# A decoder trunk on one core: the six matmuls of a dense chunk, ordered by column half in place of halves in turn

## Chip, cores and metric

The kernel runs on one NeuronCore of one Trainium2 chip. The metric is the device time of one execution in microseconds (us), smaller is better. The time before is the median of three runs, 2590.06 us (2585.79 to 2590.27).

## What is computed

One inference step of a two-layer trunk, on 512 prompt tokens and 8 x 4 new tokens of running sequences, width 1024, all in float32. Cut to what matters:

```python
for l in range(DEPTH):                                # 2 layers
    x = x + 0.5 * swiglu(rmsnorm(x), ffn1)            # 1024 -> 2816 -> 1024
    z = rmsnorm(x) @ w_in[l]                          # 1024 -> 3144
    # three head groups read z: short convolution, causal pooling,
    # and sparse attention with a top-k indexer (paged cache for the new tokens)
    x = x + concat(y_conv, y_pool, y_attn) @ w_o[l]   # 1024 -> 1024
    x = x + 0.5 * swiglu(rmsnorm(x), ffn2)
y = rmsnorm(x)
```

The dense products are the feed-forward networks (two per layer, each with gate, up and down), `w_in` and `w_o`.

## The kernel before, in words

All tokens, 512 + 32 = 544 of them, are the columns of every dense product (`TOK = 544`, `HT = 272`). Activations lie transposed, one chunk of 128 channels on the 128 partitions, so one output tile of 128 channels is the sum over 8 chunks (2 in the down projection) of a 128 x 128 weight block times a 128 x 544 chunk of activations. 544 columns do not fit one PSUM bank of 512 floats, so a tile is a pair of banks, the left half (columns 0 to 271) in one and the right half (272 to 543) in the next. `pair(p)` is that view; there are four pairs, p = 0 to 3.

Precision: weights and activations are split into a high and a low part of the reduced type fp32r (`w_hi`, `w_lo`, `h_hi`, `h_lo`, `act_hi`, `act_lo`). ScalarE makes the high part of a weight unit (L576), GpSimd the low part (L832), VectorE the low part of the activations (L1010, L1029). A chunk is then three products that are added up in PSUM: high weights by high activations, high weights by low activations, low weights by high activations.

The function `product` (L1273 to L1279) issues them: three products, each on two halves, six matmuls per chunk. In the code before, the outer loop runs over the products and the inner one over the halves (`hf`). Every dense product of the kernel goes through it:

- `unit_tile` (L1285): 8 chunks of one tile, for most gate and up tiles and for `w_in`.
- `gate_up` (L1318) with `again` false: the first tiles of a network, two tiles side by side, chunk by chunk as the normalised activations arrive (`h_chunk`, L1281, waits ahead of a chunk).
- `down` (L1338): 2 chunks per tile, 8 tiles per block of 256 hidden channels.
- the first tiles of `w_in`, and `out_part` for `w_o`.

A network has 11 blocks of 256 hidden channels; each block is 4 gate and up tiles of 8 chunks and 8 down tiles of 2 chunks. So one network calls `product` 11 x (32 + 16) = 528 times, `w_in` 26 x 8 = 208 times, `w_o` 8 x 8 = 64 times. Over two layers that is 2 x (2 x 528 + 208 + 64) = 2656 calls.

The order of work is written out by hand, engine by engine. Waits stand ahead of `product`, never inside it. Only the last of the six matmuls can carry an increment, of the semaphore `tiles`, and it does where the chunk is the last of its tile. The readers of a tile (L617 and L1024, L1036, L670, L1256) wait for that increment and read both halves of the pair in one instruction.

Line 1277 is the matmul in `product`, so all dense matmuls stand under that line in the profile. For each, the hardware has a weight load of its own (engine PEld) and the matmul (engine PE).

Of the kernel before, what the change touches and what calls it, by code (L numbers as in the profile page):

```python
# [175 lines left out]
def trunk(nc, a):  # L176

    ctx = ExitStack()
    with ctx:
# [1085 lines left out]
        def _(pe):  # L1265
# [6 lines left out]

            def product(out, w0, w1, xh, xl, first, last):  # L1273

                for w, x in ((w0, xh), (w0, xl), (w1, xh)):
                    for hf in range(2):
                        ins = pe.matmul(out[:, hf, :], w, x[:, HT * hf:HT * (hf + 1)],  # L1277
                                        start=first and w is w0 and x is xh, stop=last and w is w1)
                return ins  # L1279
# [5 lines left out]
            def unit_tile(c, p, ks, wait_h=None, first=True, last=True):  # L1285

                wh, wl = (w[:, c % 6, 0:P * len(ks)].rearrange("p (k n) -> p k n", k=len(ks)) for w in (w_hi, w_lo))
                for n, k in enumerate(ks):
                    if wait_h is not None:
                        h_chunk(wait_h, k)  # L1290
                    ins = product(pair(p), wh[:, n, :], wl[:, n, :], h_hi[:, k, :], h_lo[:, k, :],
                                  first and n == 0, last and n == len(ks) - 1)
                return ins
# [18 lines left out]
            def ffn(l, f):  # L1312
# [5 lines left out]
                def gate_up(i, j, c0, again):  # L1318

                    if not again:  # L1320

                        split_ready(l, ph, j, 1)
                        for k in range(KC):
                            h_chunk(nh, k)
                            for p in range(2):
                                wh, wl = (w[:, p, P * k:P * (k + 1)] for w in (w_hi, w_lo))
                                ins = product(pair(p), wh, wl, h_hi[:, k, :], h_lo[:, k, :], k == 0, k == KC - 1)
                                if k == KC - 1:
                                    ins.then_inc(tiles, 1)
                    for p in range(0 if again else 2, 4):  # L1330
                        split_ready(l, ph, j, c0 + p)
                        if again:

                            pe.wait_ge(silu_done if p < 2 else gu_done, s0 + 2 * i + p % 2 - 1)
                            pe.wait_ge(x_updates, xb + 8 * i - 11 + p)
                        unit_tile(c0 + p, p, range(KC)).then_inc(tiles, 1)

                def down(i, j, c0, final):  # L1338
                    split_ready(l, ph, j, c0 + 1)
                    pe.wait_ge(act_ready, s0 + 2 * i + 2)  # L1340
                    for c in range(KC):
                        p = c % 4
                        if c >= 4 or final:
                            pe.wait_ge(x_updates, xb + 8 * i + c - 3)
                        else:
                            pe.wait_ge(silu_done if p < 2 else gu_done, s0 + 2 * i + 3 + p % 2)
                        for m in range(2):
                            wh, wl = (w[:, (c0 + m) % 6, c * P:(c + 1) * P] for w in (w_hi, w_lo))
                            ins = product(pair(p), wh, wl, act_hi[:, m, :], act_lo[:, m, :], m == 0, m == 1)
                        ins.then_inc(tiles, 1)  # L1350
# [382 lines left out]
```

## Time and profile before

| | |
|---|---|
| median of three runs | 2590.06 us |
| the profiled execution, its own time | 2589.05 us |
| its span, first to last instruction | 2587.3 us |
| mean granted TensorE clock | 0.959 |
| PE busy, weight loads busy | 93%, 88% of the span |
| VectorE, ScalarE, GpSimd busy | 37%, 29%, 36% |
| share of L1277 in the chain that ended last | 78% |
| DMA | 264.64 MB, mean 102 GB/s |

Start from the shares of the engines, then ask the chain that ended last, which tells whose work sets the end. Busy times of matmuls overlap (each record lasts longer than the distance to the next), so the time per matmul is read from starts: a stretch of the chain and its count, or the distance between two rows of the timeline.

### The profile page before, as it was taken

What the parts mean: (1) busy time and instruction counts of PE and PEld (TensorE: products, weight loads), DVE (VectorE), ACT (ScalarE), POOL (GpSimd) and SP (SyncE); (2) the same over time, 40 slices, a digit from 0 to 9 for tenths busy, and PEclk for the clock granted to TensorE, in tenths of its full rate; (3) what the DMA queues carried; (4) which work ended last, traced back from release to release, by engine and by line L of the source; (5) the groups of instructions that cost most, each with busy time, mean ns of one, the idle gap of its engine ahead of it and who ended that gap; (6) DMA issues with size and microseconds to landing.
All of it is one profiled execution on the core that took longest, in us unless ns stands there. A gap on an engine that the chain in (4) does not pass through costs nothing.

```text
span 2587.3 us, 53036 instructions
## 1 busy us (share of the span) xinstructions
PE 2414.1 (93%) x19355; PEld 2270.0 (88%) x19355; DVE 956.6 (37%) x1714; ACT 757.7 (29%) x1140; POOL 925.2 (36%) x491
## 2 busy tenths in 40 slices
PE   4699999899988999999989999989998999999997
PEld 2699999859965899999989999987896668999996
DVE  2122222469746222222242222244984632222223
ACT  1322222342244232222242222234224433222223
POOL 0433443316600344333434433332562033444331
PEclk6899999899989999999989999989999988999998
DMA  4333332212379423222313323321236852233221
GB/s 89 95 96 96 105 95 73 61 41 80 98 230 288 128 82 89 73 89 89 98 53 106 96 83 94 90 69 50 58 97 203 268 181 64 84 97 97 73 87 45
DMA packets 340192, 264.64 MB, mean 102 GB/s; under 512 B 35086, under 2 KB 291560, under 8 KB 340040
## 3 DMA queue, kind: packets, MB, share of 16 engines
q1 hardware_dynamic: 338512, 260.14, 33.7%
q10 hardware_dynamic: 1032, 2.62, 0.9%
q8 instruction: 78, 1.28, 0.2%
q14 instruction: 58, 0.48, 0.1%
q0 software_dynamic: 512, 0.13, 0.0%
HBM read 253.12 MB, written 9.89 MB: 102 GB/s over the span
## 4 chain that ended last, share of the span: by engine, by line
PE 87%; SPq 4%; DMA 3%; DVE 2%; issue 2%; ACT 1%; DVEq 0%; ACTq 0%; POOLq 0%
PE ps L1277 78%; SPq L463 2%; DMA raw<-in_ffn_gate 2%; PE ps L1539 2%; PE ps L1459 1%; SPq L460 1%; PE ps L1638 1%; PE ps L1557 1%; PE ps L1627 1%; DVE work_p L1103 1%; DMA vp<-in_cache_v 1%; PE ps L1619 1%; PE ps L1381 1%; PE ps L1445 0%; PE ps L1596 0%
## 5 line engine op out<-in xcount | busy, mean ns | idle before, releaser
L832 POOL TENSOR_TENSOR w_lo<-raw,w_hi 128x1024 fp32r<-128x1024 f32 (+1 forms) x336 | 793.1, 2376 | 1512.3 <-ACT w_hi L576 1507.6
L1277 PE MATMUL ps<-h_hi,w_hi 128*128 128x272 f32 x3904 | 805.6, 291 | 59.8 <-DVE h_lo L1010 57.3
L1277 PE MATMUL ps<-h_lo,w_hi 128*128 128x272 f32 x3904 | 803.3, 290 | 0.8 <-DVE cat L1185 0.8
L1277 PE MATMUL ps<-h_hi,w_lo 128*128 128x272 f32 x3776 | 779.4, 288 | 0.0
L1277 PEld LDWEIGHTS ps<-h_hi,w_hi 128*128 128x128 f32 x3904 | 611.4, 190 | 62.6 <-DVE h_lo L1010 58.1
L1277 PEld LDWEIGHTS ps<-h_lo,w_hi 128*128 128x128 f32 x3904 | 616.6, 191 | 3.5 <-issue 3.5
L1277 PEld LDWEIGHTS ps<-h_hi,w_lo 128*128 128x128 f32 x3776 | 596.9, 190 | 0.0
L576 ACT ACTIVATE w_hi<-raw 128x1024 fp32r<-128x1024 f32 (+1 forms) x336 | 342.4, 1041 | 251.7 <-DMA raw<-in_ffn_gate 215.0
L1024 DVE TENSOR_TENSOR gated<-ps,silu 128x544 f32<-128x544 f32 x88 | 63.8, 724 | 917.9 <-PE ps L1277 917.9
L1036 DVE SCALAR_TENSOR_TENSOR xT<-ps,xT 128x544 f32<-128x544 f32 x352 | 255.0, 725 | 266.3 <-PE ps L1277 265.0
L1277 PE MATMUL ps<-act_hi,w_hi 128*128 128x272 f32 x1408 | 292.8, 289 | 9.5 <-DVE act_lo L1029 9.5
L1277 PE MATMUL ps<-act_lo,w_hi 128*128 128x272 f32 x1408 | 291.8, 288 | 0.0
L1277 PE MATMUL ps<-act_hi,w_lo 128*128 128x272 f32 x1408 | 289.2, 286 | 0.0
L623 ACT ACTIVATE act_hi<-gated 128x544 fp32r<-128x544 f32 x88 | 53.5, 651 | 628.5 <-PE ps L1277 593.0
L1277 PEld LDWEIGHTS ps<-act_hi,w_hi 128*128 128x128 f32 x1408 | 220.2, 189 | 10.4 <-issue 10.4
L1277 PEld LDWEIGHTS ps<-act_lo,w_hi 128*128 128x128 f32 x1408 | 222.1, 189 | 0.0
L1277 PEld LDWEIGHTS ps<-act_hi,w_lo 128*128 128x128 f32 x1408 | 221.6, 189 | 0.0
L617 ACT ACTIVATE silu<-ps 128x544 f32<-128x544 f32 x88 | 55.0, 625 | 343.2 <-PE ps L1277 343.2
L1539 PE MATMUL ps<-cst,kp 128*128 128x128 f32 x512 | 71.3, 294 | 19.1 <-DMA kp<-in_cache_k 19.1
L753 ACT ACTIVATE keysT<-ps 128x512 f32<-128x512 f32 x96 | 55.3, 597 | 102.5 <-PE ps L1539 102.5
L1539 PEld LDWEIGHTS ps<-cst,kp 128*128 128x128 f32 x512 | 60.6, 150 | 27.9 <-issue 24.4
L1126 DVE MAX8 top<-work_s 32x8 f32<-32x1032 f32 x64 | 78.4, 1224 | 10.1 <-DVE work_s L1122 1.1
(214 smaller groups left out, 1625.0 us busy)
## 6 DMA issues: line engine op xcount, KB each, us to landing
raw<-in_ffn_gate SPq DMA_DIRECT2D x88, 512.0 KB, 3.8
raw<-in_ffn_up SPq DMA_DIRECT2D x88, 512.0 KB, 4.0
raw<-in_ffn_down SPq DMA_DIRECT2D x88, 512.0 KB, 3.4
kp<-in_cache_k SPq DMA_DIRECT2D x128, 256.0 KB, 3.1
vp<-in_cache_v SPq DMA_DIRECT2D x128, 256.0 KB, 4.3
raw<-in_w_in SPq DMA_DIRECT2D x48, 512.0 KB, 3.8
raw<-in_w_o SPq DMA_DIRECT2D x16, 512.0 KB, 6.5
kipages<-in_cache_kidx SPq DMA_DIRECT2D x128, 32.0 KB, 1.8
```

The costliest lines, as they stand in the source:

```text
L460: page = sp.value_load(pt_sb[0:1, at_:at_ + 1], min_val=0, max_val=last_page)
L463: sp.dma_start(dst[:, q, :], src[l, page, :, :]).then_inc(s, 16)
L576: act.activation(w_hi[:, c % 6, 0:n], raw[:, c % 3, 0:n], ACT.Copy).then_inc(units_hi, 1)
L617: act.activation(halves(silu[:, m, :]), pair(m), ACT.Silu).then_inc(silu_done, 1)
L623: act.activation(act_hi[:, m, :], gated[:, m, :], ACT.Copy).then_inc(acthi_done, 1)
L753: act.activation(dst, ps[:, RING_BANKS[RING_NO[name] % NRB], 0:n], ACT.Copy).then_inc(ring_act, 1)
L832: pool.tensor_tensor(w_lo[:, c % 6, 0:n], raw[:, c % 3, 0:n], w_hi[:, c % 6, 0:n].bitcast(F32), ALU.subtract).then_inc(units_split, 1)
L1024: dve.tensor_tensor(halves(gated[:, m, :]), pair(2 + m), halves(silu[:, m, :]), ALU.mult).then_inc(gu_done, 1)
L1036: dve.scalar_tensor_tensor(halves(xT[:, c, :]), pair(c % 4), 0.5, halves(xT[:, c, :]), ALU.mult, ALU.add).then_inc(x_updates, 1)
L1126: dve.max(top8[0:32, 0, :], work_s[:, :]).then_inc(topk, 1)
L1277: ins = pe.matmul(out[:, hf, :], w, x[:, HT * hf:HT * (hf + 1)], start=first and w is w0 and x is xh, stop=last and w is w1)
L1539: ins = pe.transpose(ps[:, bank, P * c:P * (c + 1)], kp[slot][:, q, P * c:P * (c + 1)], ident)
```

## The change

The two loops of `product` change places. All three products of the left half are issued first, then all three of the right. The matmuls, their operands, their number, the start and stop flags of each, and the last matmul of the six are the same.

```diff
             def product(out, w0, w1, xh, xl, first, last):
 
-                for w, x in ((w0, xh), (w0, xl), (w1, xh)):
-                    for hf in range(2):
+                for hf in range(2):
+                    for w, x in ((w0, xh), (w0, xl), (w1, xh)):
                         ins = pe.matmul(out[:, hf, :], w, x[:, HT * hf:HT * (hf + 1)],
                                         start=first and w is w0 and x is xh, stop=last and w is w1)
                 return ins
```

On TensorE, the first tile of the down projection (`ps` is PSUM, `act_hi` and `act_lo` the parts of the gated activations) stood like this before, `x2` being the left and the right half:

```order
249 L1340 ISA [waits units_split]
250 L1346 REGISTER_ALU [waits act_ready]
251 L1277 MATMUL ps<-act_hi,w_hi 128x272 [waits silu_done]
252 L1277 MATMUL ps<-act_hi,w_hi 128x272
253 L1277 MATMUL ps<-act_lo,w_hi 128x272 x2
254 L1277 MATMUL ps<-act_hi,w_lo 128x272 x2
255 L1277 MATMUL ps<-act_hi,w_hi 128x272 x2
```

At the same place in the changed program:

```order
427 L1340 ISA [waits units_split]
428 L1346 REGISTER_ALU [waits act_ready]
429 L1277 MATMUL ps<-act_hi,w_hi 128x272 [waits silu_done]
430 L1277 MATMUL ps<-act_lo,w_hi 128x272
431 L1277 MATMUL ps<-act_hi,w_lo 128x272
432 L1277 MATMUL ps<-act_hi,w_hi 128x272
433 L1277 MATMUL ps<-act_lo,w_hi 128x272
434 L1277 MATMUL ps<-act_hi,w_lo 128x272
```

The waits stand where they stood. Rows 429 to 431 are the left half, rows 432 to 434 the right. The other four engines' programs are the same, row for row.

## Rows read from the trace of the kernel before

**Rows 1.** The page, busy time, share of the span and instructions of TensorE.

```profile
span 2587.3 us, 53036 instructions
...
PE 2414.1 (93%) x19355; PEld 2270.0 (88%) x19355; DVE 956.6 (37%) x1714; ACT 757.7 (29%) x1140; POOL 925.2 (36%) x491
```

**Rows 2.** The page, granted clock of TensorE in 40 slices, in tenths.

```profile
PEclk6899999899989999999989999989999988999998
```

**Rows 3.** The page, chain that ended last, by engine and by line.

```profile
PE 87%; SPq 4%; DMA 3%; DVE 2%; issue 2%; ACT 1%; DVEq 0%; ACTq 0%; POOLq 0%
PE ps L1277 78%; SPq L463 2%; DMA raw<-in_ffn_gate 2%; PE ps L1539 2%; PE ps L1459 1%; SPq L460 1%; PE ps L1638 1%; PE ps L1557 1%; PE ps L1627 1%; DVE work_p L1103 1%; DMA vp<-in_cache_v 1%; PE ps L1619 1%; PE ps L1381 1%; PE ps L1445 0%; PE ps L1596 0%
```

**Rows 4.** The chain in order of time: start us, us, what.

```profile
84.67 386.66 PE ps L1277 x3072
...
579.67 72.36 PE ps L1277 x576
```

**Rows 5.** L1277 by operands: count, duration ns min/median/max, first and last start us.

```profile
L1277 PE MATMUL ps<-h_hi,w_hi x3904: 283/288/596, 84.7 to 2533.3; 128*128 128x272 f32 x196
...
L1277 PE MATMUL ps<-h_lo,w_hi x3904: 282/288/595, 85.3 to 2533.5; 128*128 128x272 f32 x196
...
L1277 PE MATMUL ps<-h_hi,w_lo x3776: 282/286/432, 85.7 to 2533.8; 128*128 128x272 f32 x199
...
L1277 PE MATMUL ps<-act_hi,w_hi x1408: 286/288/428, 135.2 to 2559.9; 128*128 128x272 f32 x176
...
L1277 PE MATMUL ps<-act_lo,w_hi x1408: 283/288/428, 135.4 to 2560.2; 128*128 128x272 f32 x176
...
L1277 PE MATMUL ps<-act_hi,w_lo x1408: 282/286/428, 135.7 to 2560.4; 128*128 128x272 f32 x176
...
L1277 PE MATMUL ps<-h_lo,w_lo x128: 286/289/428, 852.7 to 2145.3; 128*128 128x272 f32 x128
```

**Rows 6.** Timeline of PE inside a down projection: start us, us, what.

```profile
1000.33 0.41 PE L1277 MATMUL ps<-act_lo,w_hi 128*128 128x272 f32 x2
1000.58 0.41 PE L1277 MATMUL ps<-act_hi,w_lo 128*128 128x272 f32 x2
1000.83 0.42 PE L1277 MATMUL ps<-act_hi,w_hi 128*128 128x272 f32 x2
1001.09 0.41 PE L1277 MATMUL ps<-act_lo,w_hi 128*128 128x272 f32 x2
1001.34 0.41 PE L1277 MATMUL ps<-act_hi,w_lo 128*128 128x272 f32 x2
```

**Rows 7.** One stretch: us, busy (count) of each engine, granted clock, DMA.

```profile
950.00:1250.00 300.00, 300.00 (x2402) 300.00 (x2402) 69.52 (x97) 70.81 (x85) 123.58 (x52) 1.00 0.30 91
```

**Rows 8.** Timeline of PE in the first chunks of `w_in`, granted clock 0.50.

```profile
498.69 0.66 PE L1277 MATMUL ps<-h_lo,w_hi 128*128 128x272 f32 x2
499.15 0.66 PE L1277 MATMUL ps<-h_hi,w_lo 128*128 128x272 f32 x2
499.60 0.66 PE L1277 MATMUL ps<-h_hi,w_hi 128*128 128x272 f32 x2
```

**Rows 9.** Timeline of PE in the index scores, 344 columns, then the line's durations.

```profile
576.33 3.05 PE L1464 MATMUL ps<-srelu,wsel 128*32 128x344 f32 x10
...
L1464 PE MATMUL ps<-srelu,wsel x24: 449/452/453, 576.0 to 1821.7; 128*32 128x344 f32 x24
```

**Rows 10.** Timeline of PE in the key transposes, 128 columns, then the line's durations.

```profile
766.15 1.04 PE L1539 MATMUL ps<-cst,kp 128*128 128x128 f32 x8
...
L1539 PE MATMUL ps<-cst,kp x512: 272/273/449, 708.7 to 2053.7; 128*128 128x128 f32 x171
```

**Rows 11.** What PE waited for: us in total, times, longest us.

```profile
PE ps L1277 <- DVE h_lo L1010: 57.3, 6, 44.7
...
PE ps L1277 <- DVE act_lo L1029: 9.5, 4, 2.4
```

## The prediction

> **What bounds the kernel now.** I read the shares of the engines first. TensorE is busy 93% of the span, and it has as many weight loads as matmuls, 19355 of each [rows 1]. A busy share alone can be an engine that waits in the right places, so the chain that ended last comes next: 87% of it is TensorE, and line 1277, the matmul of `product`, has 78% by itself [rows 3], some 2010 us. Whatever changes the time of one of these matmuls changes the time of the kernel, nearly one for one.
>
> How many are they? The seven groups by operands add up to 3 x 3904 - 128 + 3 x 1408 + 128 = 15936 [rows 5], which is 6 x 2656, the calls of `product` counted in the code.
>
> How long is one? Not the 288 ns of its record: records overlap. In the timeline of a down projection each pair of matmuls starts 0.25 or 0.26 us after the one ahead [rows 6], so 125 ns each. Over 300 us at full clock there are 2402 of them, 124.9 ns [rows 7]. The first 3072 of the chain take 386.66 us, 125.9 ns with the few waits among them, and the 576 of `w_in` take 125.6 ns [rows 4]. I call this distance from start to start the pitch. At half clock (1.2 GHz) pairs start 0.45 or 0.46 us apart [rows 8], 227 ns each, which is 272 columns at one per cycle, 226.7 ns, and nothing on top. At full clock (2.4 GHz) 272 columns would be 113.3 ns, so 11.7 ns of the pitch are something else. The clock is at 0.8 or more in every slice but the first, mostly at 0.9 [rows 2], so 125 ns is the figure that counts.
>
> The change can act only through the pitch, or through a wait that moves. **The waits first.** Line 1277 waits for VectorE's low part of the activations, 57.3 us in 6 waits, 44.7 us of which is the start of the kernel, and for the low part of the gated activations, 9.5 us in 4 [rows 11]. All of them stand ahead of a chunk and not between its six matmuls. The low part of the activations is needed by the second matmul now and not by the third, but the wait ahead of the first already covers it. The other end is the same too: the sixth matmul is still low weights by the right half, its increment comes after all six, and no reader takes the left half alone. That half is complete three pitches earlier than before, not one, and nobody is told. The weight units are read until the same matmul as before, so nothing is freed earlier or later on GpSimd, ScalarE or the load queue. No instruction of another engine is added, removed or moved. Term of the waits: 0.
>
> **Number of instructions.** Six matmuls with six weight loads before and after. The loads come with the matmuls: four loads of the high block in a row were not merged before, since loads and matmuls count alike [rows 1]. Term: 0.
>
> **The pitch.** What does the new order alter between neighbours? Two things, and both have to be priced.
>
> *Banks.* Before, every matmul wrote to another bank than the one ahead: left, right, left, right, and the next chunk begins with left after right. Now it is left, left, left, right, right, right: of six steps from a matmul to the next, four stay in the bank and add to the very columns just written, and two change the bank. That makes 4 x 2656 = 10624 steps that stay. No row at fp32r shows such a step, so I bound it. The nearest row is the index scores, plain float32, whose 12 matmuls of both layers leave 24 records, two each: the four records of an output add up in one bank before the next output goes to another. Ten records there take 3.05 us; less the last one's own length, 0.452 us [rows 9], that is 9 steps of 0.289 us. The transposes, with 128 columns, eight records to a bank, take (1.04 - 0.27) / 7 = 110 ns [rows 10]. Between the two, 216 more columns cost 179 ns, 0.83 ns a column, two cycles at full clock, so a step is the columns plus about 2.5 ns, in both. The scores have 3 in 4 steps inside a bank, the transposes 7 in 8, and neither shows more than that remainder. So staying in a bank costs nothing in the nearest row, within the rounding of 0.01 us over 9 steps, about 1 ns. Over 10624 steps 1 ns is 10.6 us, either way. What these rows leave open: plain float32 takes a column every second cycle, fp32r one every cycle. The far bound is a matmul that must wait until the one ahead has written everything: 288 - 125 = 163 ns a step, 1.7 ms in all. I take 0, by the row it is nearest to, and keep 1 ns either way as the bounds for the range.
>
> *Weights.* Before, the high block was loaded four times in a row and then the low block twice, so of six steps two change the block. Now it is high, high, low, high, high, low, and four steps change it. The trace before has both kinds side by side: from the start of the pair `act_hi,w_hi` to that of `act_lo,w_hi` no step changes the block, from `act_lo,w_hi` to `act_hi,w_lo` one does, and from there to the next chunk one does. The distances are 0.26, 0.25 and, ahead of them, 0.25 us [rows 6]. A change of block costs nothing that can be seen, so I take 0, with the same bound of rounding.
> The Trainium skill has a rule that speaks against this change: "TensorE: Matmul & The Clock Gate", in the section on what each phase of a matmul is for, says that weights are loaded by an instruction apart so that one can load once and then run many matmuls against them. By that rule the old order, which keeps the high block for four matmuls, would be the cheaper one. The trace does not agree for this kernel: it shows a load for each of the 19355 matmuls.
>
> **The sum.** 2589.05 us of the profiled execution (span 2587.3 and 1.75 around it) + 0 + 0 + 0 = **2589 us**. The median of the three runs shown is 1 us above that, well inside their own spread of 4.5 us. About 0.2%, 5.2 us, is what a measurement of this kernel can tell from no change. Over 15936 matmuls that is 0.33 ns of the pitch, or 0.49 ns of each step that stays in its bank. So the forecast of no change is a strong claim on a pitch of 125.0 ns, and this is why I keep a quarter of the chance for the two sides.
>
> **The rivals.**
>
> *Faster: changing the bank is what costs.* The pitch holds 113.3 ns of columns and 11.7 ns besides, where plain float32 needs 2.5 ns besides. That leaves 9.2 ns that no row explains. If each change of bank costs it, which happens at every step before and at two of six after, four sixths of it go: 6.1 ns by 15936 is 98 us, and the time would be 2491 us. For it: the excess is real, it is absent at half clock [rows 8], and nothing in the trace names it. Against it: bank changes in the plain float32 rows cost nothing, and the weight load, which runs beside each matmul, or the read of the columns, are as good as causes, and the order leaves both as they are. Full size: 0.04. A small gain, up to 1 ns a step, for whatever reason: 0.07.
>
> *Slower: adding to the bank just written costs.* The mechanism: the sum in PSUM is read, added and written back, and the next matmul begins on the same columns while the tail of the one ahead is still on its way. Its place is the four steps of each chunk, and it decides from 0.49 ns a step on. At 1 ns, the bound of the rows, the time is 2600 us; at 5 ns it is 2642 us. For it: at one column per cycle no row shows that it is free. Against it: rows 9 and 10 do precisely this, at half the rate, and show no more than where banks change; and the columns that are added to were begun 125 ns earlier. Chance 0.11.
>
> *Slower: changing the weights is what costs.* If the 9.2 ns sat only in the steps that change the block, 2 of 6, each would cost 28 ns, and four of six would put the pitch at 134 ns: 15936 x 9.2 ns = 147 us more, 2736 us. Against it: the two kinds of step are alike [rows 6], where 28 ns would show as 0.28 beside 0.25 us. Chance 0.03, with small costs of the same kind.
>
> *The change does not do what it says.* The program has the new order on TensorE and the other engines are untouched, so this is left only as a case of no effect and belongs to the forecast.
>
> **How the numbers follow.** Forecast of the same pitch: 0.75. Faster: 0.04 + 0.07 = 0.11. Slower: 0.11 + 0.03 = 0.14. The range takes 1 ns a step either way, 10.6 us, about 2589 and 2590: 2579 to 2601 us. It holds the forecast and the small effects of both signs, and leaves out the large ones of the rivals, together under 0.15.
>
> **What would show it.** In the profile after, line 1277 should have 15936 matmuls and as many loads, at a median record of 286 to 289 ns; the stretch from 950 to 1250 us should hold about 2402 matmuls; the first 3072 of the chain should take 386 to 387 us; the timeline should show groups of one matmul 0.12 or 0.13 us apart; and the waits of line 1277 should be the same two, of the same size. I am wrong if the pitch is under 124.7 or over 125.3 ns at full clock. With a pitch near 119 ns the bank changes were the cost; if the second and third matmul of a half start late and the first of a half on time, it is the adding in one bank; if those after a change of block start late, it is the weights. If the pitch is the same and the time is not, a wait moved, and my reading of the waits is wrong.

## The result, and the profile after

The changed kernel takes 2602.20 us, median of five runs (2596.66 to 2606.38), beside 2585.79 us for the kernel before (2583.54 to 2590.27), also in five. The ratio is 1.0057, with a 95% interval of 1.0038 to 1.0077: slower by some 15 us. The forecast was no change, and 2602.2 lies just over the end of the range.

The profiled execution of the changed kernel took 2596.66 us. From its page, the span and the busy times of the engines, against [rows 1]:

```profile
span 2594.9 us, 53036 instructions
...
PE 2421.3 (93%) x19355; PEld 2281.9 (88%) x19355; DVE 954.7 (37%) x1714; ACT 757.1 (29%) x1140; POOL 925.5 (36%) x491
```

The counts are the same, and the other engines have the same work. The waits of line 1277, against [rows 11] (us in total, times, longest us):

```profile
PE ps L1277 <- DVE h_lo L1010: 58.0, 6, 45.4
...
PE ps L1277 <- DVE act_lo L1029: 9.5, 4, 2.4
```

Two smaller waits of the line, 2.5 and 0.8 us, are the same in both traces too. So no wait took the time. The stretch at full clock that held 2402 matmuls [rows 7] now holds 2381 (us, busy and count per engine, granted clock, DMA):

```profile
950.00:1250.00 300.00, 300.00 (x2381) 300.00 (x2380) 68.88 (x96) 69.50 (x84) 119.97 (x51) 1.00 0.28 86
```

That is 300 / 2381 = 126.0 ns from start to start, where it was 124.9. Taken over all distances of the feed-forward loops in the two traces, the pitch is 126.11 ns and was 125.00. A timeline of PE in the same place (start us, us, what) shows matmuls 0.12 to 0.13 us apart, one by one and no longer in pairs; the increase is a ninth of what such a row can resolve, so it can only be read from long stretches:

```profile
1000.46 0.29 PE L1277 MATMUL ps<-h_hi,w_hi 128*128 128x272 f32 x1
1000.58 0.29 PE L1277 MATMUL ps<-h_lo,w_hi 128*128 128x272 f32 x1
1000.71 0.29 PE L1277 MATMUL ps<-h_hi,w_lo 128*128 128x272 f32 x1
1000.84 0.29 PE L1277 MATMUL ps<-h_hi,w_hi 128*128 128x272 f32 x1
1000.97 0.28 PE L1277 MATMUL ps<-h_lo,w_hi 128*128 128x272 f32 x1
1001.09 0.29 PE L1277 MATMUL ps<-h_hi,w_lo 128*128 128x272 f32 x1
1001.21 0.29 PE L1277 MATMUL ps<-h_hi,w_hi 128*128 128x272 f32 x1
```

The prediction listed signs by which step starts late. None of them came. Between 950 and 1250 us of the changed kernel the distance to the second matmul of a half is 127.5 ns on average and to the third, which changes the weight block, 124.6 ns; these are the four steps that stay in a half, 126.0 ns together. The two that change the half, and the block, take 126.3 ns. So the extra time does not stand at the steps that stay or at those that change the block; the stream as a whole is slower.

The chain that ended last has the sum. Its long pieces (start us, us, what), against [rows 4], where the first of 3072 took 386.66 us and the 576 of `w_in` 72.36:

```profile
84.08 390.38 PE ps L1277 x3072
...
583.24 72.84 PE ps L1277 x576
...
915.20 389.61 PE ps L1277 x3072
...
1332.87 389.07 PE ps L1277 x3072
```

The same pieces before:

```profile
911.84 386.16 PE ps L1277 x3072
...
1327.25 386.60 PE ps L1277 x3072
...
2159.00 387.09 PE ps L1277 x3072
```

With the fourth piece after, 390.12 us, the four long pieces grew by 12.7 us together, 1559.2 against 1546.5. The pieces of `w_in` and `w_o` grew by 1.6 us in the first layer, of which the 576 have 0.48, and by 0.6 us in the second, where 24 matmuls took 4.50 us before and 3.23 us after because of the clock. Together that is 15 us in this pair of executions, and over 16 without the 24; the medians have 2602.2 - 2585.8 = 16.4.

The span of this one execution grew only by 7.6 us, because its attention stretches were luckier with the clock. From the start of the last long piece of `w_in` to that of `w_o`, which holds the attention, it took 1.0 us less in the first layer and 4.6 us less in the second. The stretches with the key and value pages, before and then after (granted clock behind the five engines):

```profile
1950.00:2100.00 150.00, 130.47 (x1370) 86.54 (x1369) 79.53 (x214) 67.36 (x165) 12.78 (x14) 0.90 0.83 257
710.00:850.00 140.00, 118.76 (x1320) 79.89 (x1318) 75.17 (x209) 65.04 (x161) 10.59 (x13) 0.91 0.86 267
```

```profile
1950.00:2100.00 150.00, 129.91 (x1428) 91.30 (x1426) 78.07 (x213) 69.74 (x172) 21.56 (x25) 0.95 0.81 255
710.00:850.00 140.00, 120.63 (x1352) 83.67 (x1350) 76.94 (x211) 65.95 (x162) 14.24 (x16) 0.96 0.84 266
```

The granted clock is 0.95 and 0.96 in place of 0.90 and 0.91. The changed line issues no matmul there, and the mean clocks of the changed kernel's five executions, 0.960 to 0.965, lie within the 0.958 to 0.978 that the kernel before had in its runs beside the experiments. So this is taken as luck of one execution; what sets it was not tested.

At half clock nothing was lost. In the first chunks of `w_in`, against [rows 8], the starts still stand 0.22 or 0.23 us apart:

```profile
501.73 0.43 PE L1277 MATMUL ps<-h_hi,w_lo 128*128 128x272 f32 x1
501.95 0.43 PE L1277 MATMUL ps<-h_hi,w_hi 128*128 128x272 f32 x1
502.18 0.43 PE L1277 MATMUL ps<-h_lo,w_hi 128*128 128x272 f32 x1
502.41 0.43 PE L1277 MATMUL ps<-h_hi,w_lo 128*128 128x272 f32 x1
502.63 0.43 PE L1277 MATMUL ps<-h_hi,w_hi 128*128 128x272 f32 x1
```

From 501.73 to 502.63 are four steps, 225 ns each within the rounding. The 22 steps in a row from 501.50 us on, at half clock, take 226.7 ns each, and so do 19 in the trace before: the 226.7 ns of 272 columns. So the loss is 1.1 ns per matmul, at full clock alone.

### The profile page after: what moved, and what is told of

The parts are those of the page before. It is cut to its first block, busy times and chain, and to the rows that moved or that the text cites. A ratio compares the mean times of both kernels' runs of the same rounds, so it can differ in the third digit from the quotient of the medians.

```text
span 2594.9 us, 53036 instructions
## 1 busy us (share of the span) xinstructions
PE 2421.3 (93%) x19355; PEld 2281.9 (88%) x19355; DVE 954.7 (37%) x1714; ACT 757.1 (29%) x1140; POOL 925.5 (36%) x491
## 4 chain that ended last, share of the span: by engine, by line
PE 86%; SPq 5%; DMA 3%; DVE 2%; issue 2%; ACT 1%; DVEq 0%; ACTq 0%; POOLq 0%
PE ps L1277 78%; SPq L463 2%; DMA raw<-in_ffn_gate 2%; PE ps L1539 1%; SPq L460 1%; PE ps L1459 1%; PE ps L1638 1%; DVE work_p L1103 1%; DMA vp<-in_cache_v 1%; PE ps L1627 1%; PE ps L1381 1%; PE ps L1557 1%; PE ps L1445 0%; PE ps L1619 0%; DVE sq L986 0%
## 5 line engine op out<-in xcount | busy, mean ns | idle before, releaser
L1277 PE MATMUL ps<-h_hi,w_hi 128*128 128x272 f32 x3904 | 1114.0, 292 | 60.6 <-DVE h_lo L1010 58.0
L1277 PE MATMUL ps<-h_lo,w_hi 128*128 128x272 f32 x3904 | 1107.3, 290 | 0.8 <-DVE cat L1185 0.8
L1277 PE MATMUL ps<-h_hi,w_lo 128*128 128x272 f32 x3776 | 1099.6, 291 | 0.0
L1277 PEld LDWEIGHTS ps<-h_hi,w_hi 128*128 128x128 f32 x3904 | 734.3, 190 | 63.3 <-DVE h_lo L1010 58.9
L1277 PEld LDWEIGHTS ps<-h_lo,w_hi 128*128 128x128 f32 x3904 | 735.3, 190 | 2.6 <-issue 2.6
L1277 PEld LDWEIGHTS ps<-h_hi,w_lo 128*128 128x128 f32 x3776 | 717.4, 190 | 0.0
L1277 PE MATMUL ps<-act_hi,w_hi 128*128 128x272 f32 x1408 | 409.4, 291 | 9.5 <-DVE act_lo L1029 9.5
L1277 PE MATMUL ps<-act_hi,w_lo 128*128 128x272 f32 x1408 | 408.7, 290 | 0.0
L1277 PE MATMUL ps<-act_lo,w_hi 128*128 128x272 f32 x1408 | 406.4, 289 | 0.0
L1277 PEld LDWEIGHTS ps<-act_hi,w_hi 128*128 128x128 f32 x1408 | 266.0, 189 | 10.3 <-issue 10.3
L1277 PEld LDWEIGHTS ps<-act_lo,w_hi 128*128 128x128 f32 x1408 | 266.6, 189 | 0.0
L1277 PEld LDWEIGHTS ps<-act_hi,w_lo 128*128 128x128 f32 x1408 | 265.8, 189 | 0.0
```

## Experiments

Each kernel issues as many dense matmuls as before, and each differs from the kernel before in what the diff shows, unless it says from the changed one. The pitch is given two ways: from the matmuls counted between 950 and 1250 us, and as the mean distance over all of them in that stretch of the trace. Steps are counted around the six of a chunk, the step to the next chunk included.

### One factor at a time

The order changes three things and not two: which PSUM bank each of six matmuls in turn writes, which weight block it uses, and which activation columns it streams. `product` was written as a table so that each can be moved alone:

```diff
-                for w, x in ((w0, xh), (w0, xl), (w1, xh)):
-                    for hf in range(2):
-                        ins = pe.matmul(out[:, hf, :], w, x[:, HT * hf:HT * (hf + 1)],
-                                        start=first and w is w0 and x is xh, stop=last and w is w1)
+                seq = ((w0, xh, 0, 0), (w0, xh, 1, 0), (w0, xl, 0, 0), (w0, xl, 1, 1), (w1, xh, 0, 1), (w1, xh, 1, 1))
+                for n, (w, x, hf, bank) in enumerate(seq):
+                    begins = all(e[3] != bank for e in seq[:n])
+                    ends = all(e[3] != bank for e in seq[n + 1:])
+                    ins = pe.matmul(out[:, bank, :], w, x[:, HT * hf:HT * (hf + 1)], start=first and begins, stop=last and ends)
```

This is the first kernel, with the banks alone in the new order.

> The order of weights and of activation columns is that of before; only the PSUM bank each of the six matmuls writes is changed, to left, left, left, right, right, right. What is left out: sums of left and right columns land mixed, so the numbers are not the trunk's. Bank theory (adding to the bank just written costs, 4 of 6 steps): pitch 126.1 ns at full clock as after, time about 16 us over before. Weight theory and activation-address theory: pitch 125.0 ns, time of before within 0.2%.

The second, with the weight blocks alone:

```diff
+                seq = ((w0, xh, 0, 0), (w0, xh, 1, 1), (w1, xl, 0, 0), (w0, xl, 1, 1), (w0, xh, 0, 0), (w1, xh, 1, 1))
```

> Activation columns and banks in the order of before; only the weight blocks come as high, high, low, high, high, low, so four of six steps change the block in place of two. What is changed: one product is high by high where it was low, and one low by low, so the numbers are not the trunk's. Weight theory (each change of block costs 3.3 ns): pitch 126.1 ns, about 16 us over before. Bank theory and activation-address theory: pitch 125.0 ns, no change.

The third, with the streamed activations alone:

```diff
+                seq = ((w0, xh, 0, 0), (w0, xl, 0, 1), (w0, xh, 0, 0), (w0, xh, 1, 1), (w1, xl, 1, 0), (w1, xh, 1, 1))
```

> Weight blocks and banks in the order of before; only the streamed activations come in the order of after (high left, low left, high left, high right, low right, high right). What is changed: halves land in each other's banks and products are paired differently, so the numbers are not the trunk's. Activation-address theory (the start address of the streamed columns against the one ahead sets the pitch, since gaps between 119 and 130 ns repeat with a period of two chunks): pitch 126.1 ns, about 16 us over before. Bank and weight theories: pitch 125.0 ns, no change.

The fourth, the changed kernel with the banks put back:

```diff
+                seq = ((w0, xh, 0, 0), (w0, xl, 0, 1), (w1, xh, 0, 0), (w0, xh, 1, 1), (w0, xl, 1, 0), (w1, xh, 1, 1))
```

> The changed kernel with the banks alone put back to left, right, left, right, left, right; weights and streamed activations stay in the order of after. Sums of left and right columns land mixed, so the numbers are not the trunk's. Bank theory: pitch back to 125.0 ns, time of before. Weight and activation-address theories: pitch stays at 126.1 ns and the time about 16 us over before.

Measured, all beside the same runs of the kernel before (2586.30 us):

| kernel | us | ratio, 95% interval | mean pitch, ns |
|---|---|---|---|
| banks alone | 2587.16 | 1.0007 (0.9995 to 1.0019) | 125.00 |
| weight blocks alone | 2586.82 | 1.0003 (0.9993 to 1.0012) | 125.00 |
| streamed activations alone | 2603.17 | 1.0064 (1.0051 to 1.0077) | 126.11 |
| changed kernel, banks put back | 2603.55 | 1.0073 (1.0060 to 1.0086) | 126.11 |

The same stretch as above, of banks alone:

```profile
950.00:1250.00 300.00, 300.00 (x2402) 300.00 (x2401) 69.64 (x97) 70.79 (x85) 121.89 (x52) 1.00 0.29 89
```

of weight blocks alone:

```profile
950.00:1250.00 300.00, 300.00 (x2402) 300.00 (x2401) 69.52 (x97) 69.81 (x84) 122.50 (x52) 1.00 0.29 88
```

and of streamed activations alone:

```profile
950.00:1250.00 300.00, 300.00 (x2381) 300.00 (x2381) 68.86 (x96) 69.46 (x85) 117.10 (x51) 1.00 0.29 88
```

2402, 2402, 2381. Neither the banks nor the weights cost anything. The order of the streamed columns costs all of it, with banks and weights as they were.

### Tensor or half

The stream changes in two ways with the new order. It goes to the other tensor (high to low activations or back) at four of six steps, where it was two. And it stays in the same half of the columns at four of six, where it was none. Two orders that keep the sums right take these apart.

```diff
+                seq = ((w0, xh, 0, 0), (w0, xl, 1, 1), (w1, xh, 0, 0), (w0, xh, 1, 1), (w0, xl, 0, 0), (w1, xh, 1, 1))
```

> All sums are right, in another order: high by high left, high by low right, low by high left, high by high right, high by low left, low by high right. The streamed activations change between the high and the low tensor at four of six steps, as after, while the halves take turns at every step, as before. Tensor theory (a change between the high and the low activations is what costs): pitch 126.1 ns, about 16 us over before. Half theory (a stream that starts in the same half as the one ahead is what costs, 4 of 6 steps after, none before): pitch 125.0 ns, no change.

```diff
+                seq = ((w0, xh, 0, 0), (w1, xh, 0, 0), (w0, xl, 0, 0), (w0, xl, 1, 1), (w0, xh, 1, 1), (w1, xh, 1, 1))
```

> All sums are right: left half first, as after, but the two products of the high activations stand together (high left, high left, low left, low right, high right, high right), so the tensor changes at two of six steps, as before, and four of six steps stay in a half, as after. Tensor theory: pitch 125.0 ns, time of before. Half theory: pitch 126.1 ns, about 16 us over before.

The first took 2585.93 us, ratio 0.9996 (0.9987 to 1.0005), pitch 125.00 ns. The second took 2603.33 us, ratio 1.0060 (1.0046 to 1.0074), pitch 126.11 ns. The stretch in the first and in the second:

```profile
950.00:1250.00 300.00, 300.00 (x2403) 300.00 (x2402) 69.62 (x97) 70.58 (x85) 123.41 (x52) 1.00 0.30 91
```

```profile
950.00:1250.00 300.00, 300.00 (x2381) 300.00 (x2381) 68.88 (x96) 70.05 (x85) 119.36 (x51) 1.00 0.29 87
```

The tensor theory is out, and the half theory gave both numbers. The first also keeps the weight order of the changed kernel, so its four changes of block per chunk are free once more.

### Is it the address?

Why would a half matter? The layout tells. The buffers begin at 16512 bytes, 129 x 128, and each takes 8 x 544 x 4 = 17408 bytes per partition, 136 x 128. A chunk is 2176 bytes, 17 x 128, and a half 1088, 8.5 x 128. So every left half starts on a multiple of 128 bytes and every right half 64 behind one. In the order of before these two starts take turns at every step. In the new order four of six steps start where the stream ahead started, modulo 128. Two kernels with the order of before but other starts:

```diff
-                        ins = pe.matmul(out[:, hf, :], w, x[:, HT * hf:HT * (hf + 1)],
+                        ins = pe.matmul(out[:, hf, :], w, x[:, 256 * hf:256 * hf + HT],
```

> The order of before, but the right half streams columns 256 to 527 in place of 272 to 543, so that both halves start at the same place of a 1024-byte stretch. What is changed: right-hand columns are shifted by 16, so the numbers are not the trunk's. If the half theory is really one of start addresses (a start at the same place as the one ahead costs), every step costs now: pitch over 126.1 ns, about 126.7, 2610 us or more. Tensor theory, or a half theory without addresses: 125.0 ns.

```diff
-                        ins = pe.matmul(out[:, hf, :], w, x[:, HT * hf:HT * (hf + 1)],
+                        ins = pe.matmul(out[:, hf, :], w, x[:, 0:HT],
```

> The order of before, but both halves stream the left columns (right-hand results are those of the left, so the numbers are not the trunk's). Six of six steps start at the same place modulo 128. If the cost is 1.67 ns for each such step: pitch 126.7 ns. If it does not grow beyond four of six, as the run with the right half 16 columns early had it: 126.1 ns.

And one with an order in between:

```diff
+                seq = ((w0, xh, 0, 0), (w0, xh, 1, 1), (w0, xl, 0, 0), (w0, xl, 1, 1), (w1, xh, 1, 1), (w1, xh, 0, 0))
```

> All sums are right. The order of before but for the last two matmuls, which go right half first: two of six steps start at the same place modulo 128 bytes as the stream ahead, where before has none and after four. If each such step costs the same 1.67 ns: pitch 125.6 ns, about 8 us over before. If any of them puts the whole stream on the longer pitch (all six did no more than four): 126.1 ns, about 16 us. Tensor theory is out, so 125.0 ns would say that only a longer run of such steps counts.

The kernel with the right half 16 columns early took 2603.36 us (one run), pitch 126.11 ns between 950 and 1250 us: a longer pitch in the old order, by the start of the right half alone. It was expected over 126.1, and 2610 us or more. The one with its last two matmuls turned took 2598.95 us, ratio 1.0039 (1.0025 to 1.0052), pitch 125.56 ns, half way. The one that streams only left columns took 2595.60 us (one run), pitch 125.56 ns in that stretch, where I had 126.7 or 126.1. Its stretch, and then that of the turned order:

```profile
950.00:1250.00 300.00, 300.00 (x2391) 300.00 (x2390) 69.62 (x97) 69.73 (x84) 121.23 (x52) 1.00 0.29 87
```

```profile
950.00:1250.00 300.00, 300.00 (x2392) 300.00 (x2391) 68.89 (x96) 69.34 (x85) 118.64 (x50) 1.00 0.28 88
```

The last test leaves every instruction where it is and every column with its value. It is the changed kernel, with the low activations 64 bytes further on, so that in the new order the starts take turns again:

```diff
-        r_x, r_hhi, r_hlo = region(KC * TOK * 4), region(KC * TOK * 4), region(KC * TOK * 4)
+        r_x, r_hhi, r_hlo = region(KC * TOK * 4), region(KC * TOK * 4), region(KC * TOK * 4 + 64)
...
-        h_lo = at("h_lo", [P, KC, TOK], r_hlo, F32R)
+        h_lo = at("h_lo", [P, KC, TOK], r_hlo + 64, F32R)
...
-        r_cat = region(KC * TOK * 4)
+        r_cat = region(KC * TOK * 4 + 64)
...
-        act_lo = at("act_lo", [P, 2, TOK], r_cat + 2 * TOK * 4, F32R)
+        act_lo = at("act_lo", [P, 2, TOK], r_cat + 2 * TOK * 4 + 64, F32R)
```

(`srelu` and `sq`, which lie behind `act_lo`, move with it. The added space also moves what is allocated behind: the gated activations as a whole by 64 bytes, high and low alike, so that low stays 64 further than high, and the rest, the weights among it, by 128. The expectation names the low activations alone.)

> The changed kernel, its order of the six matmuls untouched; only the low activations (of the network inputs and of the gated ones) begin 64 bytes further on in each partition. In both kernels the left half of a high chunk starts on a multiple of 128 bytes and the right half 64 bytes behind one; with the shift this is the other way round for the low chunks, so that high left, low left, high left, high right, low right, high right takes turns at every step. If the start address modulo 128 against that of the stream ahead is the cause: pitch 125.0 ns, time of before, about 16 us under after. If it is the half, the order or the tensor as such: 126.1 ns and the time of after.

It took 2583.76 us, beside 2585.91 for the kernel before: ratio 0.9992 (0.9983 to 1.0001), pitch 125.05 ns. The stretch:

```profile
950.00:1250.00 300.00, 300.00 (x2402) 300.00 (x2401) 69.62 (x97) 70.58 (x85) 122.09 (x52) 1.00 0.29 89
```

And the same shift in the order of before:

> The order of before, with the low activations begun 64 bytes further on, as in the run that gave the new order its old time. Now high right to low left and low right to high left start at the same place modulo 128 as the stream ahead: two of six steps. If the start address against the one ahead is the cause: pitch 125.6 ns, about 8 us over before, as in the run with the last two matmuls turned. If the order of before is fast whatever the addresses: 125.0 ns and no change.

It took 2592.15 us, ratio 1.0024 (1.0012 to 1.0036), pitch 125.58 ns:

```profile
950.00:1250.00 300.00, 300.00 (x2392) 300.00 (x2391) 68.89 (x96) 71.10 (x86) 119.59 (x51) 1.00 0.29 88
```

So 64 bytes give the new order its old time back, and take a part of it from the old order. The weights, which moved by 128 bytes in both kernels, cannot by themselves make one faster and the other slower. It is the addresses of the streamed columns in their sequence, and not the order as such.

The same two traces hold a check. In `w_o` the high and the low part of a chunk lie in the same buffer (`cat_hi`, `cat_lo`), so the shift does not change how they stand to each other: there the new order still has four of six steps at the same place, and the old order none. In its dense stretch (866 to 898 us) the shifted new order ran at 125.7 ns and the shifted old order at 125.0, the other way round from the feed-forward networks. The sign is that of the addresses, though 125.7 is less than the 126.1 of the changed kernel.

What stays open is the full rule. With n of six steps starting at the same place modulo 128 as the stream ahead, the pitch in the feed-forward loops was:

| steps | kernels | pitch, ns |
|---|---|---|
| 0 | before; banks alone; weights alone; tensors switched; new order shifted | 125.0 |
| 2 | last two turned; old order shifted | 125.6 |
| 4 | after; streams alone; banks put back; tensors kept | 126.1 |
| 6 | right half 16 columns early | 125.6 in the first and fourth network, 126.1 in the second and third |
| 6 | left columns only | 126.1 in the third network, 125.6 in the others |

With up to four, the four networks of a trace agree, and the count gives the mean pitch: 0.28 ns for each, or 1.67 ns for each step when it is put down to those steps alone, which is bookkeeping, since single distances do not show it there. With six it is neither longer than with four nor the same in all four networks. Right half early, in the first and in the second network, and then left only, in the third:

```profile
100.00:400.00 300.00, 300.00 (x2391) 300.00 (x2390) 69.62 (x97) 69.54 (x84) 121.31 (x51) 1.00 0.33 96
950.00:1250.00 300.00, 300.00 (x2381) 300.00 (x2380) 68.94 (x96) 70.37 (x86) 117.61 (x50) 1.00 0.29 88
```

```profile
1400.00:1700.00 300.00, 300.00 (x2381) 300.00 (x2381) 68.94 (x96) 71.64 (x86) 118.58 (x50) 1.00 0.31 93
```

The first and the third network are the same instructions on the same addresses, for the first and for the second layer (the loop over `l`), and both kernels give them different pitches. So with six of six the addresses of the streams, of the weights and of the banks together do not fix the pitch; something that differs between the layers decides between the two levels. Nor is the start modulo 128 all there is with none of six: the kernel before has 125.0 ns in the networks and 125.3 in `w_in`. No run here settled either.

### What the pitch is made of

The prediction had 272 columns at one per cycle, 113.3 ns, and 11.7 ns of something else. Two kernels stream other numbers of columns in all chunks but the first of a tile:

```diff
-                        ins = pe.matmul(out[:, hf, :], w, x[:, HT * hf:HT * (hf + 1)],
+                        n = HT if first else 240
+                        ins = pe.matmul(out[:, hf, 0:n], w, x[:, HT * hf:HT * hf + n],
```

> Measures what the pitch of 125 ns is made of: every chunk but the first of a tile streams 240 columns in place of 272 (the last 32 of each half are left out, so the numbers are not the trunk's). If the 11.7 ns beside the columns are fixed, the pitch of those chunks is 100 + 11.7 = 111.7 ns. If each column is slower than one per cycle, 125 x 240 / 272 = 110.3 ns. If a weight load or an issue of fixed length sets the pitch, it stays at 125 ns and the time stays at that of before.

```diff
+            SPANS = (((0, 256), (256, 256)), ((0, 288), (256, 288)), ((0, 256), (256, 288)), ((0, 224), (272, 224)))
+            USUAL = ((0, 272), (272, 272))
...
+                spans = (SPANS[1] if now[0] in (1, 2) else USUAL) if first else SPANS[now[0]]
...
-                        ins = pe.matmul(out[:, hf, :], w, x[:, HT * hf:HT * (hf + 1)],
+                        c0, n = spans[hf]
+                        ins = pe.matmul(out[:, hf, 0:n], w, x[:, c0:c0 + n],
```

> Measures the pitch against the number of columns, in the order of before, with other columns left out or streamed twice in all chunks but the first of a tile (the numbers are not the trunk's): pair 0 streams 256 and 256 columns, both from a multiple of 128 bytes; pair 1 288 and 288, pair 2 256 and 288, likewise; pair 3 224 and 224, starting as before on a multiple of 128 bytes and 64 behind one. If the time goes by whole stretches of 128 bytes (272 columns touch nine, 256 touch eight, 240 touched eight and took 112.5 ns): 256 take 112.5 ns, 288 take 126, so 256 and 288 together take 119 a step, where 272 and 272 take 125. If it goes by columns (125 at 272, 112.5 at 240, so 0.39 a column): 256 take 118.7, 288 take 131.3. If a weight load is a floor, 224 take about 112, not 105.

(`now[0]` is the number of the pair.) One tile of each width, timeline of PE: the first row below and the last of its width are 36 matmuls apart (18 rows of two), at 256, 288 and 224 columns in the kernel with several widths.

```profile
1004.04 0.40 PE L1288 MATMUL ps<-h_hi,w_lo 128*128 128x256 f32 x2
...
1008.29 0.40 PE L1288 MATMUL ps<-h_hi,w_lo 128*128 128x256 f32 x2
...
1009.85 0.43 PE L1288 MATMUL ps<-h_hi,w_lo 128*128 128x288 f32 x2
...
1014.63 0.43 PE L1288 MATMUL ps<-h_hi,w_lo 128*128 128x288 f32 x2
...
1022.12 0.38 PE L1288 MATMUL ps<-h_hi,w_lo 128*128 128x224 f32 x2
...
1026.13 0.38 PE L1288 MATMUL ps<-h_hi,w_lo 128*128 128x224 f32 x2
```

256 columns take 4.25 us / 36 = 118.1 ns, 288 take 4.78 / 36 = 132.8 ns, and 224 take 4.01 / 36 = 111.4 ns. The tile of the same trace that streams 256 and 288 in turn takes 4.99 us for 40 (1015.69 to 1020.68 us), 125 ns, between the two. In the kernel with 240, 30 matmuls:

```profile
1000.63 0.39 PE L1278 MATMUL ps<-h_hi,w_lo 128*128 128x240 f32 x2
...
1004.01 0.39 PE L1278 MATMUL ps<-h_hi,w_lo 128*128 128x240 f32 x2
```

3.38 / 30 = 112.7 ns. (The two kernels took 2564.13 and 2443.60 us, one run each.)

From 256 to 288 the 32 columns cost 14.7 ns by these rows, 0.46 ns a column, and 14.4 ns, 0.45 a column, by the mean over all stretches of 36 such matmuls in the trace (118.3 and 132.7 ns). One column per cycle would be 13.3 ns. At 0.46 nothing is left for a fixed part, and at 0.45 some 3 ns are, not 11.7. The two widths both start every stream at the same place, where the pitch was seen to have two levels 0.56 ns apart; if they stood on different ones, the fixed part would move by 4 or 5 ns. So it is shown that the columns cost more than a cycle each and that the excess is not all fixed, and not that the fixed part is exactly 0. At 272 the whole pitch is 0.460 ns a column before and 0.464 after.

From 240 to 224 columns the pitch falls by 1.3 ns, where 16 columns at 0.46 ns would be 7. It stays at 111 to 113 ns, so something of a fixed length is the floor there; whether it is the weight load was not tested. The run with 240 alone could have been read as 11.7 ns of fixed part (111.7 ns expected). The time does not go by whole stretches of 128 bytes either: 240, 256 and 272 columns would be 112.5, 112.5 and 126.

## Why the prediction was wrong

**What bounds the kernel** held. Line 1277 sets the end, the number of its matmuls is 15936, and a change of the pitch went into the time nearly one for one: 1.1 ns in the feed-forward networks and somewhat less in the rest gave about 16 us.

**The term of the waits, 0,** held: the two waits that the prediction priced are 58.0 and 9.5 us, and were 57.3 and 9.5 [rows 11]. (One reading there is off without bearing on the term: the left half is complete three pitches ahead of the sixth matmul in place of one, so two pitches earlier than before.) **The number of instructions** held too, 19355 matmuls and as many loads.

**The pitch** is where it failed, at the sentence "What does the new order alter between neighbours? Two things". There is a third, the streamed operand. I priced the two I had named at 0, and the runs with the banks alone and the weights alone say that both prices were right. The term that was left out carries all: the pitch is 1.11 ns longer in the feed-forward networks, 126.11 for 125.00 ns, with four of six streams starting where the one ahead started, modulo 128 bytes. Shared out over those steps that is 1.67 ns each. Over the 12672 matmuls of the four networks 1.11 ns is 14 us, and `w_in` and `w_o`, at 0.8 to 0.9 ns, have the rest within the spread. The bounds of the range, 1 ns a step either way, were the rounding of one row of plain float32, where a column takes two cycles; they had nothing to do with the cost that was there. That the measured time fell only 1 us outside is luck of those bounds.

**The faster rival** rested on 11.7 ns "besides the columns". No such part was found: the columns themselves go at 0.45 to 0.46 ns, slower than one per cycle, which leaves some 3 ns or nothing (less surely with the two levels in mind), and with four of the six changes of bank taken away the pitch stayed at 125.00 ns. **The slower rivals** had the right sign, for wrong reasons: "adding to the bank just written" is refuted, and so is "changing the weights". The latter had also been misread: 28 ns at two steps of six would make pairs of 0.23 and 0.26 us, and not 0.25 and 0.28. [rows 6] exclude it even so, since their 0.26 us is the pair without a change of block. The Trainium skill says in "TensorE: Matmul & The Clock Gate", in the section on what each phase of a matmul is for, that weights can be loaded once for many matmuls. The run with the weights alone shows what the order of blocks costs here: with four changes of block per chunk in place of two the ratio is 1.0003, and the interval holds 1. Each of the 19355 matmuls had its own load in that run too, so what fewer loads would be worth is not shown.

The trace of before had a hint that I did not use. The distances between its matmuls are not equal: behind the 0.25 and 0.26 us of [rows 6] they run from 119 to 130 ns and repeat every two chunks. Banks repeat with every chunk, and weight blocks begin every 512 bytes, which would need a rule modulo 1024 to repeat so. The addresses of the activations do it modulo 256: two chunks of 2176 bytes are 4352, 17 x 256. It was a hint and no proof, and it is one more sign that the place modulo 128 is not the whole rule.

## What to carry to other kernels

When neighbouring instructions are reordered, list every operand of each, also the streamed one, and ask what its address is against the one ahead; a permutation of equal work is not free by itself. In a kernel bound by dense fp32r matmuls, fit the layout to the loop order, so that successive streams take turns between a multiple of 128 bytes and 64 behind one. Here each order runs at 125.0 ns in the layout that does this for it, and at 125.6 or 126.1 in the other one; the whole of it is 0.6% of the time. A pitch that is longer than its columns should be measured at two widths before it is taken apart into columns and a rest.

## What the runs showed of the hardware

- A stream of fp32r columns at full clock, with one weight load per matmul, has a pitch of 118.1 to 118.3 ns at 256 columns, 125.0 to 126.1 at 272 and 132.7 to 132.8 at 288: 0.45 to 0.46 ns a column, where one cycle is 0.42, and little or nothing fixed. At half clock it takes one column per cycle: 226.7 ns for 272.
- With one weight load of 128 columns per matmul the pitch was still 111.4 ns at 224 columns and 112.7 at 240. What the floor is was not tested.
- The start address of a stream against that of the stream ahead moves the mean pitch at 272 columns, in levels of 125.0, 125.6 and 126.1 ns, at full clock alone. Where all six steps started at the same place, the same instructions ran at 125.6 ns in one layer and at 126.1 in the other.
- Four matmuls of six that add to the bank just written cost nothing (ratio 1.0007, 0.9995 to 1.0019), and neither do four changes of the weight block of six (1.0003, 0.9993 to 1.0012).
